# Two transformer blocks on one core: interleaving the modulation chunks at the start with first K halves of the query and key panels

## The reference, cut to what matters

```python
mod   = silu(c)     @ w_ada + b_ada        # 1024 -> 6*1024; shift and scale are chunks 0,1 and 2,3
mod_c = silu(c_ctx) @ w_ada + b_ada
h  = rmsnorm(x,   g_norm1) * (1 + sc1)  + sh1
hc = rmsnorm(ctx, g_norm1) * (1 + scc1) + shc1
cq, ckv, kpe, rq, rk, rv, rg = split(h @ w_in)      # for hc too, but without cq, rq, rg
```

## Time and profile before

| | |
|---|---|
| median of 3 runs | 911.49 us (907.62 to 912.02) |
| the profiled execution | 905.98 us, span 904.2 us |
| TensorE busy | 839.9 us, 93% of the span |
| VectorE busy | 614.7 us, 68% |
| ScalarE busy | 459.1 us, 51% |
| mean granted TensorE clock | 0.985 |

### The profile page before, as it was taken

The page is one execution under the profiler, slowest core; times in us unless marked ns, Lnnn a source line. Parts: engine busy times, 40 slices in busy tenths (PEclk is TensorE's granted clock), DMA queues, the critical chain, the costliest instruction groups (busy, mean ns, idle before and its releaser), DMA issues. The chain is left out here.

```text
span 904.2 us, 13610 instructions
## 1 busy us (share of the span) xinstructions
PE 839.9 (93%) x5334; PEld 742.7 (82%) x5334; DVE 614.7 (68%) x952; ACT 459.1 (51%) x720; POOL 16.2 (2%) x21
## 2 busy tenths in 40 slices
PE   3799998799999999999998989989998899999996
PEld 2598787667899999998788967768977899999885
DVE  4956986979777777774566667558545766666543
ACT  5735365245546666664445575445644444444442
POOL 1001000000000000000000000000000000000000
PEclk9989999999999999999999999999999899999999
DMA  9932583457565666666557543225614365656641
GB/s 340 356 126 86 167 267 94 124 151 216 173 224 174 182 182 186 187 186 197 176 161 249 177 141 117 71 71 186 186 48 146 111 185 177 184 182 182 191 160 46
DMA packets 103511, 152.91 MB, mean 169 GB/s; under 512 B 6506, under 2 KB 55702, under 8 KB 103448
## 3 DMA queue, kind: packets, MB, share of 16 engines
q1 hardware_dynamic: 101160, 145.48, 51.5%
q10 hardware_dynamic: 2288, 6.57, 1.9%
HBM read 150.97 MB, written 1.05 MB: 168 GB/s over the span
## 5 line engine op out<-in xcount | busy, mean ns | idle before, releaser
L1873 DVE TENSOR_TENSOR w_lo<-raw,w_hi 128x1024 fp32r<-128x1024 f32 (+1 forms) x244 | 293.1, 1213 | 175.6 <-ACT w_hi L1367 174.7
L1367 ACT ACTIVATE w_hi<-raw 128x1024 fp32r<-128x1024 f32 (+1 forms) x244 | 252.5, 1048 | 213.9 <-PE bank L709 115.3
L784 PE MATMUL bank<-hT_hi,w_hi 128*128 128x256 f32 x864 | 245.7, 284 | 4.7 <-DVE w_lo L1873 4.4
L785 PE MATMUL bank<-hT_lo,w_hi 128*128 128x256 f32 x864 | 245.3, 284 | 0.0
L786 PE MATMUL bank<-hT_hi,w_lo 128*128 128x256 f32 x864 | 245.2, 284 | 0.0
L784 PEld LDWEIGHTS bank<-hT_hi,w_hi 128*128 128x128 f32 x864 | 166.7, 193 | 5.5 <-issue 4.2
L785 PEld LDWEIGHTS bank<-hT_lo,w_hi 128*128 128x128 f32 x864 | 166.7, 193 | 0.0
L786 PEld LDWEIGHTS bank<-hT_hi,w_lo 128*128 128x128 f32 x864 | 166.7, 193 | 0.0
L707 PE MATMUL bank<-w_hi,hT_hi 128*128 128x512 f32 (+2 forms) x224 | 87.7, 392 | 10.3 <-DVE hT_lo L1936 3.7
L709 PE MATMUL bank<-w_hi,hT_lo 128*128 128x512 f32 (+2 forms) x224 | 85.9, 383 | 0.0
L708 PE MATMUL bank<-w_lo,hT_hi 128*128 128x512 f32 (+2 forms) x224 | 85.9, 383 | 0.0
(11 more groups left out here) (332 smaller groups left out, 1190.1 us busy)
## 6 DMA issues: line engine op xcount, KB each, us to landing
raw<-w_up_dram SPq DMA_DIRECT2D x132, 256.0 KB, 3.6
raw<-w_ada_dram SPq DMA_DIRECT2D x48, 512.0 KB, 4.8
raw<-w_down_dram SPq DMA_DIRECT2D x44, 512.0 KB, 4.1
raw<-w_in_dram SPq DMA_DIRECT2D x40, 512.0 KB, 4.6
raw<-w_gate_dram SPq DMA_DIRECT2D x44, 256.0 KB, 3.2
raw<-w_out_dram SPq DMA_DIRECT2D x16, 512.0 KB, 3.4
raw<-wk_x_dram SPq DMA_DIRECT2D x8, 512.0 KB, 4.2
raw<-wv_x_dram SPq DMA_DIRECT2D x8, 512.0 KB, 3.4
```

Of the source, the lines that this page charges most:

```text
L784: pe.matmul(o, hi[:, c:c + P], xh[:, k, :], start=f, stop=False, skip_group_check=True)
L785: pe.matmul(o, hi[:, c:c + P], xl[:, k, :], start=False, stop=False, skip_group_check=True)
L1367: act.activation(unit_view(w_hi[n % NSPLIT], u), unit_view(raw[u % NRAW], u), ACT.Copy).then_inc(w_hi_ready, 1)
L1873: dve.tensor_tensor(unit_view(w_lo[n % NSPLIT], u), unit_view(raw[u % NRAW], u), unit_view(w_hi[n % NSPLIT], u).bitcast(F32), ALU.subtract ...
```

## The change

The order of the units is written out (`START_ORDER`): `ada0`, `ada2`, the first half of `cq`, three units of `ada1`, the first unit of `rk`, the last of `ada1`, `ada3`, then `rk` 1, `cq` 1, `rk` 2, `rk` 3. The turns of x and ctx are cut into pairs 0, 1 (their gains come from chunks 0 and 2) and pairs 2, 3 (chunks 1 and 3). `rk` comes ahead of `ckvpe`, and the turn of `mem` moves into `rv`. The load of ctx moves from ScalarE's queue to SyncE's, behind `ada2`; the ten small vectors of group 1 move the other way. The two tiles of `cq` share one PSUM bank, and banks at the start are named by hand. Groups 2 and 3 of the small vectors (the convolution's) are transposed and copied after the second halves of the turns. The `decay` table is made after the turn of `mem`, no longer before it.

The core of the diff (renumberings of norms and semaphores' counts are left out):

```diff
 
-ADA_ORDER = [0, 1, 2, 3]
+ADA_ORDER = [0, 2, 1, 3]
+
+
+START_ORDER = ([("ada0", n) for n in range(4)] + [("ada2", n) for n in range(4)]
+               + [("cq", 0), ("ada1", 0), ("ada1", 1), ("ada1", 2), ("rk", 0), ("ada1", 3)]
+               + [("ada3", n) for n in range(4)] + [("rk", 1), ("cq", 1), ("rk", 2), ("rk", 3)])
...
+    for name, n in START_ORDER:
+        _, kind, kt, nk, cols, sources = by_name[name]
+        add_unit(name, n * nk, nk, cols, sources, kind)
+    started = {name for name, _ in START_ORDER}
     for name, kind, kt, nk, cols, sources in panels:
...
-                m = modrow[:, p % 2, :]
+                m = modrow[:, ADA_ORDER.index(p) % 2, :]
...
             pe.wait_ge(c_lo_ready, 2)
-            for p in range(4):
-                ada(p)
-                if p:
-                    ada_spread(p - 1)
-                else:
-                    for g in range(1, len(VEC_GROUPS)):
-                        turn_vectors(g)
-            ada_spread(3)
-            turn("x1")
-
             cT = (hcT_hi, hcT_lo)
-            cq = rows_steps("cq", hT_hi, hT_lo, turn_before("x1"), b=0)
+            ada0, ada2 = ada_steps(0, 0), ada_steps(2, 1)
+            next(ada0)
+            turn_vectors(1)
+            run(ada0)
+            next(ada2)
+            next(ada2)
+            ada_spread(0, 5)
+            run(ada2)
+            turn("x1", None, range(2), (6, 7))
+            ada_spread(2, 5)
+            cq = cq_steps()
             next(cq)
-            turn("ctx")
+            ada1 = ada_steps(1, 5)
+            next(ada1)
+            next(ada1)
+            turn("ctx", None, range(2), (6, 7))
+            next(ada1)
+            rk = rows_steps("rk", hT_hi, hT_lo, turn_before("x1"), cT, b=0, ctx_before=turn_before("ctx"))
+            next(rk)
+            run(ada1)
+            ada3 = ada_steps(3, 6)
+            next(ada3)
+            next(ada3)
+            ada_spread(1, 7)
+            run(ada3)
+            turn("x1", None, range(2, 4), (7, 5))
+            ada_spread(3, 6)
+            next(rk)
+            turn("ctx", None, range(2, 4), (7, 5))
+            for g in range(2, len(VEC_GROUPS)):
+                turn_vectors(g, 6)
             run(cq)
-            rows_panel("ckvpe", hT_hi, hT_lo, turn_before("ctx"), cT, b=4)
-            rk = rows_steps("rk", hT_hi, hT_lo, None, cT, b=0)
-            for _ in range(3):
-                next(rk)
+            run(rk)
+            rows_panel("ckvpe", hT_hi, hT_lo, None, cT, b=4)
+            rv = rows_steps("rv", hT_hi, hT_lo, None, cT, b=0)
+            next(rv)
             turn("mem")
-            run(rk)
-            rows_panel("rv", hT_hi, hT_lo, None, cT, b=4)
-            rows_panel("rq", hT_hi, hT_lo, b=0)
-
-            for name in ("cq", "ckv", "ckvc"):
-                turn(name)
+            run(rv)
+            rows_panel("rq", hT_hi, hT_lo, b=4)
+
+            for name, b in (("cq", 6), ("ckv", 7), ("ckvc", 0)):
+                turn(name, banks=(b, b))
             rows_panel("rg", hT_hi, hT_lo, b=2)
+            small[0] = 1
...
-                if u == NRAW - 1:
-                    for group, done in ((1, in_vec), (2, in_conv), (3, in_conv)):
+                if u == last_unit["ada2"]:
+                    sp.dma_start(in_ctx[:, :, :], a["ctx"].rearrange("(t p) d -> p t d", p=P)).then_inc(in_ctxx, 16)
+                if u == first_unit["rk"]:
+                    for group, done in ((2, in_conv), (3, in_conv)):
                         for name, _ in VEC_GROUPS[group]:
                             g, r, n = VEC[name]
...
             act.dma_start(k0[:, :], const[:, 0:C_RCOS]).then_inc(in_ident, 16)
-            act.dma_start(in_ctx[:, :, :], a["ctx"].rearrange("(t p) d -> p t d", p=P)).then_inc(in_ctxx, 16)
+            for name, _ in VEC_GROUPS[1]:
+                g, r, n = VEC[name]
+                act.dma_start(vrow[g][r:r + n, :], vec_src[name]).then_inc(in_vec, 16)
             act.dma_start(res[:, :, :], a["x"].rearrange("(t p) d -> p t d", p=P)).then_inc(in_x, 16)
...
+            act.wait_ge(in_x, 16)
+            square("x1", 0, 0, res[:, 0, :])
+            feed_units(5)
+            square("x1", 0, 1, res[:, 1, :])
+            feed_units(6)
+            ada(0)
+            feed_units(8)
+            scale_row("x1", res[:, 1, :], row[:, 1, :])
+            feed_units(10)
+            ada(2)
+            turn("x1", None, range(2))
+            feed_units(11)
             act.wait_ge(in_ctxx, 16)
             square("ctx", 0, 0, in_ctx[:, 0, :])
-            feed_units(6)
             square("ctx", 0, 1, in_ctx[:, 1, :])
-            feed_units(7)
-            ada(0)
-            feed_units(8)
-            act.wait_ge(in_x, 16)
-            square("x1", 0, 0, res[:, 0, :])
-            feed_units(10)
-            square("x1", 0, 1, res[:, 1, :])
-            feed_units(11)
+            feed_units(12)
+            scale_row("ctx", in_ctx[:, 1, :], in_ctx[:, 1, :])
+            turn("ctx", None, range(2))
+            feed_units(16)
             ada(1)
-            feed_units(13)
-            scale_row("ctx", in_ctx[:, 1, :], in_ctx[:, 1, :])
-            feed_units(15)
-            ada(2)
-            scale_row("x1", res[:, 1, :], row[:, 1, :])
             feed("ada3")
             ada(3)
-            turn("x1")
-            turn("ctx")
+            turn("x1", None, range(2, 4))
+            feed_one()
+            turn("ctx", None, range(2, 4))
...
             feed("cq")
+            use = ("cq", 0)
+            ready(act, use)
+            free(act.activation(cq_row[:, :, :], ps(use)[:, :].rearrange("p (t d) -> p t d", t=T), ACT.Copy), use)
+            emptied(act, use)
             for t in range(T):
...
+            feed_one()
...
+            feed("rk")
+            act.wait_ge(in_mem, 16)
+            for t in range(T):
+                square("mem", 0, t, row[:, t, :])
+            feed("ckvpe")
...
             scale_row("mem", row[:, 1, :], row[:, 1, :])
             feed_one()
             turn("mem")
-            feed("rk")
             feed("rv")
...
-                    if before:
-
-                        dve.wait_ge(turn_lo, before)
+                    if fbuf_free[name, p]:
+
+                        dve.wait_ge(turn_lo, fbuf_free[name, p])
...
+                ps_ = list(pairs or range(kt // 2))
                 feed_units(min(fed[0] + 1, limit))
                 if scaled:
-                    full(0)
-                for p in pairs or range(n):
-                    if scaled and p + 1 < n:
-                        full(p + 1)
+                    full(ps_[0])
+                for n, p in enumerate(ps_):
+                    if scaled and n + 1 < len(ps_):
+                        full(ps_[n + 1])
                     rest(p)
                     if p in (1, 2):
                         feed_units(min(fed[0] + 1, limit))
+                    if between is not None and n == 0:
+                        between()
...
+            def gains_of(p):
+
+                some = slice(4 * p, 4 * p + 4)
...
+            columns(1)
+            feed_units(5)
+            variance("x1")
+            feed_units(7)
+            spread(0)
+            feed_units(8)
+            scale_rows("x1", [res[:, 0, :]], [row[:, 0, :]])
+            feed_units(9)
+            spread(2)
+            gains_of(0)
+            turn("x1", None, range(2))
+            feed_units(11)
             variance("ctx")
-            for g in range(1, len(VEC_GROUPS)):
+            scale_rows("ctx", [in_ctx[:, 0, :]], [in_ctx[:, 0, :]])
+            feed_units(12)
+            turn("ctx", None, range(2), lambda: feed_units(13))
+            feed_units(16)
+            spread(1)
+            feed("ada3")
+            spread(3)
+            gains_of(1)
+            turn("x1", None, range(2, 4))
+            feed_units(fed[0] + 1)
+            turn("ctx", None, range(2, 4))
+            for g in range(2, len(VEC_GROUPS)):
                 columns(g)
...
+            variance("cq")
+            scale_rows("cq", [cq_row[:, t, :] for t in range(T)], [cq_row[:, t, :] for t in range(T)])
             feed("rk")
+            dve.wait_ge(in_k1, 16)
             for t in range(T):
                 rope_ret(("rk", t), t, rk_row)
-            feed_units(fed[0] + 1)
+            feed_units(min(fed[0] + 1, reach(last_unit["ckvpe"] + 1)))
             dve.wait_ge(wctx_ready, 8)
             for t in range(T):
                 use = ("rk", T + t)
@@ -2102,7 +2138,41 @@
                         ins = dve.tensor_scalar(dst[:, t, h * P:(h + 1) * P], ps(use)[:, h * P:(h + 1) * P],
                                                 wctx[:, d, h, t:t + 1], RET_SCALE, ALU.mult, ALU.mult)
                 free(ins, use)
-                feed_units(fed[0] + 1)
+                feed_units(min(fed[0] + 1, reach(last_unit["ckvpe"] + 1)))
+            variance("mem")
+            feed("ckvpe")
+            scale_rows("mem", [row[:, 0, :]], [row[:, 0, :]])
```

(63 more changed lines are left out.)

109 lines of the change are left out of this document (41 added, 68 removed).

## The result

The changed kernel is **slower by 2.2%**: the ratio of the two kernels' times is 1.0218, with a 95% interval of 1.0194 to 1.0242. So it is slower beyond doubt, but whether by more than 2% is not quite clear. The medians are 928.15 us (926.73 to 929.21) against 909.56 for the kernel before in the same session (905.92 to 912.02), which is +18.6 us (by the ratio it would be 19.8), where the forecast had +11.2. It is just past the 928 at which the stated range ends. The profiled execution of the changed kernel took 928.81 us, its span is 927.0, 22.8 longer than the span before.

A forecast was written before the change was run, and what follows sets the result against it. TensorE's matmuls set the pace from 57 to 94 us, not ahead of 57. Early waits and low clock move the turn of `cq` from 128.4 to 139.6: +11.2, 917.2 profiled, 922.7 median; range 910 to 928.

The forecast's parts named there:

- wait for bank 6: TensorE, between transposes of vector groups 2 and 3: new wait of 4.5 us until VectorE copies group 2.
- E: Point where the turn of `cq` begins, same work done in both kernels: forecast 139.6 us, against 128.4 before.
- wait of `rv` 3: TensorE ahead of `rv`'s last unit: 2.6 us, for VectorE's conversion behind the turn of `mem`, bounds and `decay`.
- Past E ... I count nothing: After the turn of `cq` begins: list the same but for banks, VectorE's list sets that stage, +0 us.
- the chain from `rk` 0 to S: Conversions, last modulation units, spreads and hand-overs from the end of `rk` 0 to the last spread's end: 10.15 us.
- the clock behind the last wait: Behind the 2.6 us wait at `rv` 3: between 0 and 3.1 us more, taken as 0, being shorter, in dense work.
- The start: Up to the first half of `cq`: ScalarE's 11.15 us chain from about 12.8; added issues cost 0.3 at most, counted nothing.
- rival 3: From 140 to 200 us later waits give half the loss back: +5 us, 916.5 or less; chance 0.15.
- Rival 1: Clock holds at `rk` 0 and `cq` 1, losing 3.1 and 2.7 from the sum: +5.4 us, 916.9; chance 0.22.
- Rival 2: Moved halves fill TensorE's holes free in the modulation, last spread near 44: -5.7 us, 905.8; chance 0.10.
- Rival 4: Low clock also behind the last wait, at `rv` 3: +14.3 us, 925.8; chance 0.06.
- the prediction's +7: Low-clock terms of 3.1, 3.1 and 2.7 early in the kernel could each be about half in one run: sum some +7.

The follow-up runs named there:

- experiment 9: Changed kernel with one claim of bank 6 for vector groups 2 and 3, and `rv` 3's conversion ahead of `decay`: 1.0070 to the kernel before.
- experiments 1 to 5: Changed kernel, singly: one bank 6 claim 1.0112; `rv` 3's conversion before `decay` 1.0140; `rk` 0 behind modulation 1.0162; early holes overfilled 1.0192; filled with less 1.0145.
- experiments 7 to 10: Changed kernel, one bank 6 claim and `rv` 3 before `decay`; first two also `rk` 0 behind modulation; second, fourth with holes filled: 1.0055, 1.0022, 1.0070, 1.0029.
- experiment 7: Changed kernel with one bank 6 claim, `rv` 3's conversion before `decay`, and `rk` 0 behind the last modulation unit, no filling: 1.0055 to the kernel before.

## Why the prediction was right and where it failed

**Right: the direction, and what makes it.** All the waits it named came, in its order and with the releasers that it named.

| step | forecast | first trace |
|---|---|---|
| `cq` 0 starts, idle before it | 29.3, 4.1 | 30.54, 4.15 |
| `cq` 0 takes | 5.15 | 5.1 |
| `rk` 0 starts, idle before it | 42.0, 3.4 | 43.69, 3.59 |
| `rk` 0 takes | 8.6 | 8.3 |
| from its end to the last spread's (S) | 10.15 | 11.7 |
| wait for bank 6 | 4.5 | 4.87 |
| from S to the end of `rk` | 28.0 | 27.8 |
| from the end of `rk` to E | 50.8 | 53.4 |
| in it, wait of `rv` 3 | 2.6 | 3.50 |
| E | 139.6 | 144.96 |
| behind E | +0 | +6.3 |

**Wrong: the size, and the step is "Past E ... I count nothing", with the sum up to E too small as well (its start, the chain from `rk` 0 to S, and the clock behind the last wait "taken as 0").** By the two pairs of traces E moved by 16.5 and 13.2, mean 14.9, where the sum had 11.2; behind E came 6.3 and 0.7 more, mean 3.5, where it had nothing. Together 18.4, near the 18.6 of the medians.

*Up to E* both traces of the changed kernel run late against the sum at the same three places.

1. *The start*, 1.2 us. ScalarE's chain of 11.15 us up to the second copy took 12.1 in the first trace and began 0.3 later than assumed, which is the added issues' bound. It also stood 0.40 us for the load of x and 0.50 for TensorE's last unit of `ada2`, neither of which is in the sum.
2. *From `rk` 0 to S*, 1.6 us: 11.7 in both traces for 10.15. The clock was low from 59 to 63 (58 to 61 in the second trace), behind waits of 0.60 and 1.46 that I took for harmless. In the trace of experiment 9, where it was at 1.00 there, the same stretch took 11.05; so 0.7 is the clock, and 0.9 is missing in the chain that I summed, in which link stays open.
3. *From the end of `rk` to E*, 2.6 us, all at `rv` 3: its wait was 0.9 longer than the 2.6 of the sum, and the 3.4 us at the low level behind it, "taken as 0", cost 1.7.

`rk` 0 itself took 8.3 and 7.4 where the sum had 8.6. In all, E came at 144.96 and 143.40 for 139.6; against it, the second trace of the kernel before has its own E 1.8 later than the first. The clock's part of the forecast's 11.2 is about 5 (2.25 for `cq` 0, 3.1, 2.7, less the 3.1 of before). Measured were 7.4 and 3.1, mean 5.3. That this agrees is in part luck: the sum had neither the stretch at 59 nor the one at 126, and the stretches that it counted in full came short in the second trace. The idle time grew by 9.1 and 10.1, where the forecast had some 6.2. Two readings of the kernel before were off without changing the sum: its stretches of low clock behind the two long waits are 6.8 us each, not 6.4, and the wait behind its turn of `mem`, ahead of the first unit of `rv`, is 1.56, not 1.9.

*Behind E* the idle time is level (41.2 and 41.0 before, 40.5 and 40.5 after), so **rival 3**, that later waits take half up, fell: they took up half a microsecond. The difference is TensorE's busy time at 4803 matmuls: 734.6, 737.2 and 736.5 in the three traces of the kernel before and its filled form, 738.3 to 741.6 in the seven of the changed kernel and experiments 1 to 5. But of experiments 7 to 10, which have the same program behind E, 7 and 8 have 741.6 and 739.9, and 9 and 10 have 736.4 and 737.7, inside the range of before or 0.5 from it. So the order of the work behind E does not by itself bring the slow matmuls. One part of it has a place: the matmuls behind `rkT`, 3.43 us at 164.75 with the clock low, take 2.05 at full clock in the kernel before. Their wait is 2.15 in the changed kernel with 1.13 ahead of it, where the kernel before has 1.76 with 1.60. The clock was low there in both traces of the changed kernel and in experiments 1 to 5 and 7, and full in 8, 9 and 10, with nearly the same waits. So these waits do not decide it alone, and why the changed kernels fall into it more often stays open.

**Rival 1** (the clock holds at `rk` 0 and `cq` 1) fell, both had 3.4 or 6.8 us at the low level. **Rival 2** (a free filling) fell: S is at 63.7, far from 49.7, since panel units hold the operand buffers; ScalarE's wait of 7.90 us shows it. **Rival 4** (low clock behind the last wait too) is what happened; I had given it 0.06, for dense work behind a short wait, against which all six traces with the 3.5 us wait speak. That its 925.8 lies nearest to the measured 928.15 is partly luck, since that stretch cost 1.7 and not 3.1, and the rest came from places that it did not have.

The stretch behind `cq` 0's hole was 6.8 us in the first trace of the changed kernel and 3.4 in the second, and so was the one behind `rk` 0's. The page "TensorE: Matmul & The Clock Gate" of the Trainium skill, section "What's actually happening", says of the slow matmuls at a kernel's start that their number varies from run to run and should not be fitted; the prediction carried this over to stretches in the middle of a kernel, and these two traces agree with it there. It does not make the sum small, though, as the prediction's +7 had it: E moved by 13.2 in the second pair too. There were five low stretches up to E in each trace of the changed kernel, where the sum counts three.

**What the parts cost**, by undoing them: the second claim of bank 6 1.1% and `decay` ahead of `rv` 3 0.8%, both with the clock behind them and 1.5% together; the place of `rk` 0 some 0.1% once these are gone, which is inside the noise; the clock behind the two early holes 0.3 to 0.4% more. What remains of the change, all repaired and filled, is 1.0022 against 0.9983 for the kernel before with its own hole filled. The other parts of the change (`cq` 0 inside the modulation with the turns cut in two, `rk` ahead of `ckvpe`, the moved loads) were not undone one by one. Whether a fourth operand buffer would make the interleaving pay was not tried.

## What to carry to other kernels

Count a wait on TensorE at its own length and the slow matmuls behind it, also for a wait of 3.5 us in dense work. Take one trace's clock for a draw: compare idle time and busy time apart, profile twice, and look at the mean clock of all runs. Before units of another product are put between the units of a chunk that gates the rest, look at who holds the operand buffers: here the gate moved from 39.9 to 63.7 us and every list behind it was reordered against its old cover. Two transposes that share a bank go under one claim, and a conversion that TensorE waits for goes ahead of work that nobody waits for yet.

## What the runs showed of the hardware

Granted clock: two executions of one program differ by 14 us in the time at the low level (65.5 and 51.9; 26.7 and 40.3); the part behind E differs by 3.2 and 2.3 us with it. Fifty runs of the kernel before have 27 to 49 us. Stretches come as 3.4 or 6.8 us, seldom longer (10.2 in the second trace before, 13.7 in experiment 7). A wait of 3.5 us in dense work (`rv` 3) had one behind it in six traces of six. The wait of 1.46 behind the spread of `ada1`, with thin work around it, had one in ten traces of eleven (in one of them the clock was low already). One of 1.53 to 1.56 in dense work (the first unit of `rv` in the kernel before) had none in three. Filling 3.1 of 4.15 us of a hole with constant matmuls left 1.03 of it and kept the clock at 1.00. This gained 0.3 to 0.7% in the changed kernels, and 0.2% in the kernel before, where the interval reaches zero. A filling matmul of 128x256 in float32 was two instructions: 7 calls are x14 in 3.27 us, 0.47 a call, where `cq`'s matmuls of 256 columns on rounded operands take 0.12 at full clock.
